# Retention stage of a hybrid encoder block: chunk products ordered from both ends, decayed values moved ahead of two square sums, row norms divided between ScalarE and VectorE, and four weight roundings moved in between the probabilities' copies

## What is computed

```python
def retention_scan(q, k, v, log_gamma, strict):      # chunks of 128 tokens
    s = einsum('bhncd,bhnmd->bhncm', q, k) * dmask
    intra = einsum('bhncm,bhnme->bhnce', s, v)
    kv = einsum('bhncd,bhnce->nbhde', k_dec, v)       # one 128x128 product a chunk
    _, prev = lax.scan(step, zeros, kv)               # state * chunk_decay + kv_n
    return intra + einsum('bhncd,nbhde->bhnce', q_dec, prev)
...
y = y_f + y_b                                         # forward and reversed scan, 4 heads of 128
yn = (y - mean(y)) * rsqrt(var(y) + EPS) * gn_w       # per token and head
r = silu(g) * yn
mix = concatenate([a, r]) @ w_out                     # a: normed attention rows
...
p = softmax(q @ k_mem); xo = (p @ v_mem) @ xa_wo      # cross-attention, 4 heads
```

## Time and profile before

| | us |
|---|---|
| median of 3 runs (lowest to highest) | 1433.22 (1432.66 to 1433.55) |
| the profiled execution, its own time | 1433.89 |
| span of the profiled execution | 1431.7 |
| PE busy | 1398.8 (98%) |
| DVE, ACT, POOL busy | 845.9, 640.6, 821.0 |

### The profile page before, as it was taken

One profiled execution on the slowest core, in us unless ns is written; L12 is line 12 of the kernel. 1 busy time (PEld: TensorE's weight loads), 2 busy tenths in 40 slices (PEclk: granted clock), 3 DMA queues, 4 the chain that ended last, 5 costly groups with the idle time before them and its releaser, 6 DMA issues.

```text
span 1431.7 us, 18919 instructions
## 1 busy us (share of the span) xinstructions
PE 1398.8 (98%) x6744; PEld 1152.4 (80%) x6744; DVE 845.9 (59%) x1273; ACT 640.6 (45%) x1299; POOL 821.0 (57%) x579
## 2 busy tenths in 40 slices
PE   7999999998999999999999999999999999999998
PEld 7988888666978888887888888888888888868886
DVE  4699996786875767855256633333333333343868
ACT  6422233676533765354366433333333333534454
POOL 1587255002862755510344687777777774799753
PEclk9999999999999999999999999999999999999999
DMA  5577232100034364210536133332332324933463
GB/s 198 164 241 235 60 95 67 60 1 1 31 107 158 118 227 142 90 44 6 189 96 224 38 111 111 111 111 96 111 103 96 111 81 174 362 88 88 107 209 148
DMA packets 127309, 172.17 MB, mean 120 GB/s; under 512 B 9584, under 2 KB 73328, under 8 KB 127216
## 3 DMA queue, kind: packets, MB, share of 16 engines
q1 hardware_dynamic: 123776, 161.52, 34.5%
q10 hardware_dynamic: 3440, 9.45, 1.8%
HBM read 129.77 MB, written 41.16 MB: 119 GB/s over the span
## 4 chain that ended last, share of the span: by engine, by line
PE 81%; DVE 5%; POOL 5%; DMA 4%; ACT 2%; issue 2%; SPq 1%; POOLq 0%; DVEq 0%; ACTq 0%
PE ps L1127 24%; PE ps L1129 23%; PE ps L1128 23%; PE ps L1123 5%; PE ps L1532 2%; DVE z L2834 1%; PE ps L1295 1%; PE ps L1389 1%; POOL wd L1096 1%; POOL w_lo L927 1%; PE ps L1323 1%; DMA gain_b<-f_rows 1%; PE ps L1367 1%; DMA z_sums<-z 1%; DVE sm L2709 1%
## 5 line engine op out<-in xcount | busy, mean ns | idle before, releaser
L1127 PE MATMUL ps<-w_hi,t_hi 128*128 128x512 f32 (+2 forms) x592 | 229.2, 387 | 4.5 <-POOL w_lo L1016 2.6
L1129 PE MATMUL ps<-w_hi,t_lo 128*128 128x512 f32 (+2 forms) x592 | 226.8, 383 | 0.0
L1128 PE MATMUL ps<-w_lo,t_hi 128*128 128x512 f32 (+2 forms) x592 | 226.0, 382 | 0.0
L1127 PEld LDWEIGHTS ps<-w_hi,t_hi 128*128 128x128 f32 x592 | 112.7, 190 | 25.2 <-POOL w_lo L1016 3.2
L927 POOL TENSOR_TENSOR w_lo<-raw,w_hi 128x512 fp32r<-128x512 f32 (+1 forms) x52 | 79.8, 1542 | 91.0 <-ACT w_hi L1818 91.0
L1129 PEld LDWEIGHTS ps<-w_hi,t_lo 128*128 128x128 f32 x592 | 112.6, 190 | 20.0
L1128 PEld LDWEIGHTS ps<-w_lo,t_hi 128*128 128x128 f32 x592 | 112.7, 190 | 19.0
L1016 POOL TENSOR_TENSOR w_lo<-raw,w_hi 128x512 fp32r<-128x512 f32 x32 | 41.6, 1318 | 103.9 <-ACT w_hi L2190 103.8
L3153 DVE TENSOR_TENSOR ev<-ps,ev 128x512 f32<-128x512 f32 x21 | 14.5, 692 | 144.2 <-PE ps L1129 144.2
L1818 ACT ACTIVATE w_hi<-raw 128x512 fp32r<-128x512 f32 (+1 forms) x52 | 31.6, 619 | 107.5 <-PE ps L1129 65.2
L2383 ACT ACTIVATE ev<-ps 128x512 f32<-128x512 f32 x63 | 37.7, 598 | 88.6 <-PE ps L1129 88.6
(11 more groups left out here) (368 smaller groups left out, 4081.2 us busy)
## 6 DMA issues: line engine op xcount, KB each, us to landing
raw_a<-in_ffn_w_gu_dram SPq DMA_DIRECT2D x44, 256.0 KB, 3.2
raw_b<-in_ffn_w_gu_dram SPq DMA_DIRECT2D x44, 256.0 KB, 3.2
f_rows<-fs SPq DMA_DIRECT2D x44, 256.0 KB, 3.6
gain_b<-f_rows SPq DMA_DIRECT2D x39, 256.0 KB, 2.7
tables<-f_rows SPq DMA_DIRECT2D x38, 256.0 KB, 2.7
f_rows<-fa SPq DMA_DIRECT2D x33, 256.0 KB, 3.4
raw<-in_xa_wkv_dram SPq DMA_DIRECT2D x32, 256.0 KB, 3.4
raw<-in_xa_wo_dram SPq DMA_DIRECT2D x32, 256.0 KB, 2.6
```

The source lines that it names most:

```text
L1127: nc.tensor.matmul(out, a_hi, b_hi, start=start, stop=False, skip_group_check=onto)
L1128: nc.tensor.matmul(out, a_hi, b_lo, start=False, stop=False, skip_group_check=onto)
L1129: return nc.tensor.matmul(out, a_lo, b_hi, start=False, stop=stop, skip_group_check=onto)
```

## The change

It does four things. (1) PE makes the chunk products in the order 0, 1, 7, 6, 2, 3, 5, 4, and the recurrences wait for them by that order. (2) `decayed_values(2)` stands ahead of the third of the first four square sums, in place of behind the fourth. (3) Of the four heads' norms DVE keeps heads 0 and 1 (16 instructions), ACT does heads 2 and 3 (16 instructions that need -mean/root, which DVE makes in one more instruction of 32 columns); POOL's `mix(t)` waits for both, and three mixes stand ahead of `low_part(5)`, five behind it, then `low_part(6)` and `(7)`. (4) `xo_round` 4 to 7 are taken in between `probs_high` 4 to 7.

```diff
+CHUNKS_BOTH_WAYS = (0, 1, 7, 6, 2, 3, 5, 4)
...
             def mix(t):
 
-                pool.wait_ge(r_n, 1 + RH * (t + 1))
+                pool.wait_ge(r_n, 2 + 2 * (t + 1))
+                pool.wait_ge(r_rt, 1 + 2 * (t + 1))
...
             low_part(4)
+            for t in range(3):
+                mix(t)
             low_part(5)
-            for t in range(5):
+            for t in range(3, NT):
                 mix(t)
             low_part(6)
-            for t in range(5, NT):
-                mix(t)
             low_part(7)
...
-                for n in range(NT):
+                for n in CHUNKS_BOTH_WAYS:
                     nc.tensor.matmul(ps[:, 2 + n // 2, (n % 2) * 256:(n % 2 + 1) * 256],
...
                     for t in range(4 * h, 4 * h + 4):
+                        if t == 2:
+                            decayed_values(2)
                         square_root(NT + t, z[:, t, 0:512], junk_c[:, 0:512], 512, lambda: act.wait_ge(w_a, t + 1))
-                    decayed_values(h + 2)
+                    if h == 1:
+                        decayed_values(3)
...
+            def normed(t):
+
+                act.wait_ge(r_n, 2)
+                for h in range(2, RH):
+                    v, i = z[:, t, C_RQ + h * RD:C_RQ + (h + 1) * RD], h * NT + t
+                    nc.scalar.activation(v, v, ACT.Identity, bias=rsd[:, i:i + 1], scale=rrs[:, i:i + 1]).then_inc(r_rt, 1)
+
+            for t in range(4):
+                normed(t)
             round_out(5)
+            for t in range(4, NT):
+                normed(t)
             round_out(6)
...
-            for t in range(4, NT):
-                probs_high(t)
+            probs_high(4)
+            probs_high(5)
+            xo_round(4)
+            xo_round(5)
+            probs_high(6)
+            xo_round(6)
+            probs_high(7)
+            xo_round(7)
...
-            for n in range(RING, 12):
+            for n in range(NK, 12):
                 xo_round(n)
...
-                        dve.wait_ge(r_kv, NT * h + n // 2 * 2 + 2)
+                        dve.wait_ge(r_kv, NT * h + CHUNKS_BOTH_WAYS.index(n) // 2 * 2 + 2)
...
             dve.wait_ge(r_n, 1)
+            nc.vector.scalar_tensor_tensor(out=rsd[:, :], in0=mv[:, :, 0], scalar=-1.0, in1=rrs[:, :], op0=ALU.mult,
+                                           op1=ALU.mult).then_inc(r_n, 1)
             for t in range(NT):
-                for h in range(RH):
+                for h in range(2):
```

## The result

| | before | after |
|---|---|---|
| median of 9 runs each, us (lowest to highest) | 1433.22 (1430.92 to 1439.37) | 1426.59 (1425.16 to 1429.94) |
| profiled execution: own time, span, us | 1433.89, 1431.7 | 1427.07, 1425.3 |

After to before: 0.9958, 95% interval 0.9946 to 0.9969. The median fell by 6.6 us and the span by 6.4.

The account below looks back on a forecast made before the run. PE, busy for 98% of the 1431.7 us span, was taken as the bound, so only its waits count. Heads +0.1, norms and mixes -1.8, roundings -4.5 sum to -6.2: from 1433.22 to 1427.0 us, range 1424.8 to 1429.8.

Parts of the forecast that it names:

- Head 2 earlier: Retention heads on PE: head 2's chunk products would start at 363.23 us, 1.88 us earlier.
- What comes back: Head 3: POOL's earlier multiplication blocks a DVE attention norm, states come late, outputs 3 start at 383.8, 0.1 us later.
- A: Length on PE from head 0's score products to outputs 3, 39.01 us before; forecast to change by +0.1 us.
- Rival (a): Head 3: POOL's multiplication does not collide with the norms; the heads give -1.9 us, time 1425.0; chance 0.17.
- Rival (b): Outputs 3's wait costs more: two norms blocked (+2.7), or clock drops (up to 1.7 us); 1428.7 to 1429.6; chance 0.14.
- Part 3: Norms and mixes: PE's last transposes in quarter 0 no longer wait for POOL's mixes, -1.77 us.
- rival (c): Clock falls in quarter 0 anyway, or ACT (a table load) eats some norms gain; 1428.5 to 1430; chance 0.10.
- Part 4: Roundings: PE's wait at unit 4 goes (-2.84 us) and the clock stays up (1.71 us), together -4.5 us.
- C: Length on PE from quarter 0's last transposes to unit 4, 3.63 us before; forecast change -2.84 us.
- D: Length on PE from unit 4 to the product behind unit 7, 12.68 us before; forecast change -1.71 us.
- A2: Length on PE from outputs 3 to the first half product, 8.32 us before; forecast change 0.

Follow-up runs that it names:

- e2: The kernel before with only the two-ended chunk order and the earlier decayed values: 1432.45 us, ratio 0.9996.
- e4: The changed kernel, with POOL's query multiplication for head 3 also waiting until the sixth attention norm is done: 1423.88 us, ratio 0.9934 to the kernel before.
- e9: The changed kernel without the two-ended chunk order, with POOL's head 3 multiplication waiting for six attention norms: 1425.53 us, ratio 0.9945.
- e5: The changed kernel with chunk products again in order 0 to 7, decayed values still earlier: 1426.61 us, ratio 0.995.
- e11: The changed kernel, with POOL's query multiplication for head 3 waiting for five attention norms (e4 with five in place of six): 1428.35 us in one run.
- e3: The kernel before with only the norms divided between DVE and ACT and the mixes regrouped: 1431.13 us, ratio 0.9983.
- e7: The kernel before with only POOL's list changed, all eight mixes ahead of `low_part(6)`, all norms on DVE: 1431.36 us, ratio 0.9994.
- e6: The kernel before with only the decayed values earlier: 1430.98 us, ratio 0.9987.
- e10: The kernel before with only the two-ended chunk order: 1433.66 us, ratio 1.0007.

## Why the prediction was right, point by point

Forecast 1427.0 us, measured 1426.59.

- **Head 2 earlier** (decayed values earlier). Forecast 363.23. Measured 362.91; with the 0.32 us that everything in the trace is earlier, 363.23. e2 gives the same 1.88 us.
- **What comes back.** POOL's multiplication was forecast at 373.73, measured 373.41 + 0.32 = 373.73; the norm's end at 376.9, measured 376.59 + 0.32 = 376.91; outputs 3 at 383.8, measured 383.77, and +0.04 us against +0.1. This was the step without a row of its own: that L945 blocks L2820 as L954 does. The trace now has that row, 2.65 us against 0.75, and e4 and e9 show that it is the cause and not a neighbour: without the meeting A is 1.9 and 1.3 us shorter than before. The Trainium skill ("SBUF — State Buffer", "Who interferes with whom") has it that two SBUF inputs on VectorE meet any GpSimd instruction that reads SBUF; these rows agree. It also says that whoever issues first gets the shared pair. In the changed kernel (0.34 us) that holds; in e5 and e11 the norm's row begins 0.04 and 0.03 us first and the norm loses.
- **Rival (a)** (no collision, 1425.0) is e4's kernel: with the collision taken away the heads give -1.86 us, where it said -1.9. e4's median, 1423.88, is 1.1 us under that forecast; 1.36 us of its profiled execution's gain on the one before stand ahead of A, so this part is no merit of the edit. Rival (a) also called 0.5 us of delay on POOL enough; e11 bears on this. There POOL stands 0.55 us later behind head 0's score products than in the changed kernel (29.56 against 29.01), beside an unchanged norm, and the norm is still blocked. That margin was set too low.
- **Rival (b).** Its second half did not happen in the profiled execution, where the clock stayed at 1.00 behind the wait of 1.76 us, and did in e11 behind one of 2.03. Two of the nine runs of the changed kernel lie at 1429.6 and 1429.9, which such a drop would explain. The granted clock of the whole run is 0.998 in the first, 0.999 in the second and in the seven others, so the drop is likelier in the first; they have no trace, and this stays open. The forecast drew on the page's row of clocks for there being no drop at the three other waits. That row can't show one: it has a 9 in every slice, the slice of unit 4 too. The reading is right all the same, for the view by stretches has 1.00 before from 353 to 358, from 365 to 369 and from 418 to 423 us.
- **Part 3.** -1.78 against -1.77. Its inside was off by one price: ACT's norm takes 480 ns and not 386, 0.386 us from start to start (3.19 us for 8) and not 0.30. The row that I took has one operand that is a column of the tile, this instruction has two. The Trainium skill ("ScalarE: Activation LUTs", "What ACT_TABLE_LOAD costs") gives 186 ns + 0.833 a column + about 93 for each such operand, which makes 479; the trace agrees. The wrong price cost nothing: each group of 8 took 3.19 us in place of 2.5, but ACT still stood idle for 0.22 us before PE released the rounding of unit 5, and the last mix ended at 413.17, where PE needed it 7 x 0.45 us after 413.92. The mixes kept ahead by more than forecast: the last was to end at 414.3. The first of ACT's norms starts 0.04 us after DVE's -mean/root is over (399.74), and ACT's timeline has no table load between the root and the norms (rival (c)).
- **Part 4.** C is the forecast -2.84. The clock gave 1.61 and not 1.71. By D the same term is 1.50 in e2 and 1.76 in e3 and e7, so 1.71 lies within its scatter; in e6 it is 2.90. How much of this term one execution gives back is in part luck.
- **Left out of the forecast:** A2's +0.08. It stands where outputs 3 had to wait for the states (e2, e5, e6, and e4, there for 0.02 us), and not where they were ready (e3, e9, e10): the first pair behind a wait takes 0.46 us in place of 0.39, as e4's row shows.

## What to carry to other kernels

An edit that frees one engine also moves the meetings on a shared port. Before paying for "PE is 1.9 us earlier", list what else that releases, and look whether it falls on a two-input instruction of DVE that a later result depends on; if it does, one wait on the engine that has slack is worth more than the edit itself: here POOL's two instructions start 1.4 us later and end 0.7 us later, for 1.9 us of gain. And when the gain looked for is 1 us in 1430, read it from a length between two starts in the trace: e7's 1.04 and e4's 1.90 us are plain there, and near or below what ratios of whole runs can tell.

## What the runs showed of the hardware that was not expected

- **A row that begins first does not always win.** A 128x512 norm of two inputs lost to POOL with a start 0.03 us ahead in e11 (2.93 us) and 0.04 us ahead in e5 and e6 (2.94 us), and won with 0.34 us (0.75 us). When it lost, it was over 0.55 us after POOL's end, while alone it takes 0.75. One reading is that the lock is taken inside the row, and that the first 0.2 us of the norm (an estimate from these rows) need none; another is that POOL has the lock before its row begins, or gives it up before the row ends. The runs don't tell these apart, nor where between 0.04 and 0.34 us the limit lies.
- **What the same idle time does to the clock differs.** The waits of 2.60 us ahead of unit 4 were followed by a stretch at half clock in every one of the six traces that had them: D was 12.57, 12.68, 12.69, 12.83 and 12.83 us in e2, before, e10, e3 and e7, and 13.97 in e6, against 11.07 without, so that one and the same wait cost 1.5 to 2.9 us on top of itself. It need not cost that at all: one of e6's runs without a trace (1431.14 us) has a mean granted clock of 1.000, where one stretch as in the earlier trace rows would leave 0.9988 at most. For e6 the view by stretches has 0.51 over 6.9 us, where the earlier trace rows have 0.62 over 4.5:

```profile
677.50:684.40 6.90, 6.16 (x15) 4.81 (x16) 0.00 (x0) 1.47 (x3) 4.38 (x4) 0.51 0.52 154
```

  A wait of 2.03 us at outputs 3 brought it down in e11, one of 1.99 at chunk products 2 left it at 1.00 in e10, in the same view:

```profile
363.90:368.00 4.10, 4.10 (x21) 3.69 (x22) 4.06 (x21) 4.00 (x12) 4.10 (x3) 1.00 0.00 0
```
